# Token rows gathered as half rows on 128 partitions, and a mixture-of-experts loop whose first weight piece is used in two halves

## The reference, cut to what matters

```python
logits = x2 @ w_router + b_router
top_v, top_i = lax.top_k(logits, 4)
gates = softmax(top_v)
# the 1280 (token, expert) pairs are sorted by expert and padded to blocks;
# for every block of rows xb with its expert e:
gu = xb @ w_gu[e] + b_gu[e]                     # (rows, 1024) @ (1024, 2048)
gate = minimum(gu[:, :1024], 7.0)
up = clip(gu[:, 1024:], -7.0, 7.0)
hid = (up + 1.0) * gate * sigmoid(1.702 * gate)
y = hid @ w_dn[e] + b_dn[e]                     # (rows, 1024) @ (1024, 1024)
# out[token] += y * gate of the pair
```

## Time and profile before

| what | us |
|---|---|
| median of 3 runs | 1650.93 |
| lowest and highest run | 1648.24 and 1654.43 |
| the profiled execution, its own time | 1646.45 |
| its span in the profile | 1644.6 |
| TensorE busy | 1488.4 (91%) |
| expert phase: first token transpose to the last down piece | 567.0 to 1617.4 |

### The profile page before, as it was taken

One profiled execution on the slowest core, in us unless ns is written; L12 is line 12 of the kernel. 1 busy time (PEld: TensorE's weight loads), 2 busy tenths in 40 slices (PEclk: granted clock), 3 DMA queues, 4 the chain that ended last, 5 costly groups with the idle time before them and its releaser, 6 DMA issues.

```text
span 1644.6 us, 20052 instructions
## 1 busy us (share of the span) xinstructions
PE 1488.4 (91%) x6990; PEld 690.1 (42%) x6991; DVE 338.2 (21%) x786; ACT 327.9 (20%) x603; POOL 123.5 (8%) x227
## 2 busy tenths in 40 slices
PE   9999999999999898878899988788999886998882
PEld 6676666766774432222233322222333222332221
DVE  3655422333211520100111101001011010011005
ACT  3534423443101111111111111111111110111011
POOL 0200000000000000000010100000101000011000
PEclk9999999999999999989999999899999998999897
DMA  7222132212743499999989999999899999579997
GB/s 271 91 92 79 63 111 79 78 51 103 255 154 154 159 368 413 418 416 409 417 306 376 387 415 416 413 411 418 313 362 397 412 415 404 238 270 407 409 422 233
DMA packets 92391, 477.23 MB, mean 290 GB/s; under 512 B 13015, under 2 KB 16972, under 8 KB 43202
## 3 DMA queue, kind: packets, MB, share of 16 engines
q1 hardware_dynamic: 84040, 461.14, 70.8%
q0 software_dynamic: 7920, 15.45, 2.9%
q10 hardware_dynamic: 394, 0.15, 0.0%
HBM read 471.47 MB, written 15.18 MB: 296 GB/s over the span
## 4 chain that ended last, share of the span: by engine, by line
PE 72%; DMA 20%; DVE 3%; issue 3%; SPq 1%; ACT 0%; ACTq 0%; DVEq 0%; POOL 0%; POOLq 0%
PE bank L622 28%; PE bank L1054 20%; DMA ring<-in_w_gate_up 19%; PE bank L1080 16%; PE bank L626 3%; PE bank L1060 1%; DVE r_kv L1491 1%; DVE r_v L1494 1%; PE bank L903 1%; SPq L579 1%; SPq L586 0%; DMA y_rows<-r_xt,r_qk 0%; PE bank L778 0%; DVE r_c L1494 0%; DVE r_qk L1488 0%
## 5 line engine op out<-in xcount | busy, mean ns | idle before, releaser
L1054 PE MATMUL bank<-ring,r_kv 128*64 128x512 f32 x2128 | 510.3, 627 | 99.5 <-DMA ring<-in_w_gate_up 98.8
L1054 PEld LDWEIGHTS bank<-ring,r_kv 128*64 128x64 f32 x2128 | 153.0, 143 | 401.5 <-issue 296.0
L1080 PE MATMUL bank<-ring,r_kv 128*64 128x512 f32 x1216 | 283.5, 609 | 0.7 <-ACT r_kv L1164 0.7
L622 PE MATMUL bank<-r_xt,ring 128*128 128x320 f32 (+2 forms) x848 | 241.7, 440 | 0.9 <-ACT r_o L1164 0.9
L1488 DVE TENSOR_SCALAR r_kv<-bank 128x512 f32<-128x512 f32 (+1 forms) x78 | 53.6, 687 | 913.2 <-PE bank L1060 911.9
L622 PEld LDWEIGHTS bank<-r_xt,ring 128*128 128x128 f32 x848 | 158.3, 190 | 71.0 <-issue 5.0
L1080 PEld LDWEIGHTS bank<-ring,r_kv 128*64 128x64 f32 x1216 | 90.8, 144 | 193.8 <-issue 192.9
L1164 ACT ACTIVATE r_xt<-bank 128x512 f32<-128x512 f32 x38 | 22.7, 597 | 513.7 <-PE bank L1080 513.7
L1434 ACT ACTIVATE r_o<-r_kv 128x512 f32<-128x512 f32 x38 | 24.0, 632 | 310.3 <-DVE r_kv L1488 310.3
L626 PEld LDWEIGHTS bank<-const,r_v 64*128 64x128 f32 (+3 forms) x512 | 48.4, 156 | 75.0 <-DVE r_v L1494 42.8
L1060 PE MATMUL bank<-ring,r_kv 128*64 128x512 f32 x304 | 71.6, 592 | 0.0
(11 more groups left out here) (258 smaller groups left out, 907.5 us busy)
## 6 DMA issues: line engine op xcount, KB each, us to landing
ring<-in_w_gate_up SPq DMA_DIRECT2D x256, 1024.0 KB, 18.6
ring<-in_w_down SPq DMA_DIRECT2D x128, 1024.0 KB, 14.9
ring<-in_w_in SPq DMA_DIRECT2D x12, 2048.0 KB, 8.4
ring<-in_w_proj_b SPq DMA_DIRECT2D x2, 2048.0 KB, 9.1
ring<-in_w_proj_a SPq DMA_DIRECT2D x2, 2048.0 KB, 9.8
ring<-in_w_out SPq DMA_DIRECT2D x2, 2048.0 KB, 8.0
ring<-y_rows SPq DMA_DIRECT2D x8, 512.0 KB, 11.3
ring<-in_w_uq SPq DMA_DIRECT2D x2, 1152.0 KB, 9.2
```

The costliest lines, as they stand in the source:

```text
L622: ins = pe.matmul(out, l, r, start=(n == 0), stop=(n == len(pairs) - 1), **kw)
L1054: ins = pe.matmul(half(gate_bank if q < 2 else up_bank, q % 2), xg[:, k, :], w[:, 512 * q:512 * q + 512], start=False, stop=False, skip_gr ...
L1080: ins = pe.matmul(half(out_bank, t), hidT[:, 2 * (j % 2) + s, BLK * h:BLK * h + BLK], w[:, s, 512 * t:512 * t + 512], start=(j == 0 and s ...
```

## The change

Four things are changed together.

- **The gather.** `xrow` becomes 128 partitions by 512 columns. Slot s has the first half of its row on partition s and the second half on partition 64 + s; the index table gets one entry for every partition (2 times the token, plus 1 for the upper 64), and the gather takes rows of 2 KB.
- **The token transposes.** 4 transposes of 128 by 128 take the place of 8 of 64 by 128. The bank then holds, for each of four 128-column groups, the slots' lower half and upper half side by side; `xg` is indexed by (k % 4, k // 4), so that every matmul still reads 64 adjacent columns.
- **The order on TensorE.** Behind `bias`, the two gate matmuls of piece 0 (`first_gate`, with the waits for `m_xg` and for the weights) stand ahead of `hidden_turned`, and its two up matmuls (`first_up`) behind it.
- **`pick` on VectorE** is made at the start of a turn, when piece 0 of the block is through, and no longer between `gt` and `up`.

```diff
-        xg = r3(r_kv[:, 0:512], 8)
+        xg = r_kv[:, 0:512].rearrange("p (k h s) -> p k h s", k=4, h=2)
-        xrow = r_v[0:BLK, 1216:2240]
+        xrow = r_v[:, 1216:1728]
+        x_halves_dram = x_rows_dram.rearrange("t (h d) -> (t h) d", h=2)
...
-                for k in range(8):
-                    ins = turn(xt_bank[:, BLK * k:BLK * k + BLK], xrow[:, 128 * k:128 * k + 128])
+                for k in range(4):
+                    ins = turn(xt_bank[:, 128 * k:128 * k + 128], xrow[:, 128 * k:128 * k + 128])
...
+            def first_gate(e):
+                pe.wait_ge(up_in[0], 16 * e + 16)
+                for t in range(2):
+                    pe.matmul(half(gate_bank, t), xg[:, 0, 0, :], up_w(0)[:, 512 * t:512 * t + 512],
+                              start=False, stop=False, skip_group_check=True)
+            def first_up():
+                for t in range(2):
+                    ins = pe.matmul(half(up_bank, t), xg[:, 0, 0, :], up_w(0)[:, 1024 + 512 * t:1536 + 512 * t],
+                                    start=False, stop=False, skip_group_check=True)
+                ins.then_inc(m_up, 1)
...
                 bias(b + 1)
+                pe.wait_ge(m_xg, b + 2)
+                first_gate(e1)
                 hidden_turned(b)
-                pe.wait_ge(m_xg, b + 2)
-                gate_up(0, e1)
+                first_up()
...
             with dve.Fori(0, nb) as b:
+                dve.wait_ge(m_up, 8 * b + 1)
+                ts(pick, lane, be[:, bass.ds(dve.snap(b + 1), 1)], ALU.is_equal).then_inc(m_pick, 1)
                 dve.wait_ge(m_gate, b + 1)
                 ts(gt, banks[2][:, :], LIMIT, ALU.min).then_inc(m_gt, 1)
-                ts(pick, lane, be[:, bass.ds(dve.snap(b + 1), 1)], ALU.is_equal).then_inc(m_pick, 1)
...
-                pool.indirect_dma_start(xrow, None, x_rows_dram[:, :],
-                                        bass.IndirectOffsetOnAxis(ap=column[0:BLK, :].bitcast(U32), axis=0),
-                                        bounds_check=NQ - 1, oob_is_err=False).then_inc(m_xrow, 16)
+                pool.indirect_dma_start(xrow, None, x_halves_dram,
+                                        bass.IndirectOffsetOnAxis(ap=column.bitcast(U32), axis=0),
+                                        bounds_check=2 * NQ - 1, oob_is_err=False).then_inc(m_xrow, 16)
```

More of the change, by code:

```diff
@@ L51 @@
                   ("mask", NT), ("expert", NE), ("block", NB1), ("lane", 1),
-                  ("slot", BLK), ("thr", 6), ("pad", 3), ("tok4", 12)]:
+                  ("slot", BLK), ("thr", 6), ("pad", 4), ("tok4", 12)]:
     CONST_AT[_name] = (_at, _n)
@@ L86, in constants @@
     put("tok4", TOPK * (first + p - NQ))
-    put("pad", np.concatenate([TOPK * NQ + p % BLK, 2 * (TOPK * NQ + p % BLK) + p // BLK,
-                               np.where(p % BLK, 2 * NQ, NQ - 1)], axis=1))
+    put("pad", np.concatenate([TOPK * NQ + p % BLK - 1.5, 2 * (TOPK * NQ + p % BLK) + p // BLK,
+                               np.where(p % BLK, 16 * NQ, TOPK * (NQ - 1)), p // BLK], axis=1))
     return c
@@ L1053, in gate_up @@
                     for q in range(4):
-                        ins = pe.matmul(half(gate_bank if q < 2 else up_bank, q % 2), xg[:, k, :],
+                        ins = pe.matmul(half(gate_bank if q < 2 else up_bank, q % 2), xg[:, k % 4, k // 4, :],
                                         w[:, 512 * q:512 * q + 512], start=False, stop=False, skip_group_check=True)
@@ L1059, in gate_up @@
                     for t in range(2):
-                        ins = pe.matmul(half(bank_, t), xg[:, 7, :], w[:, 512 * (q0 + t):512 * (q0 + t) + 512],
+                        ins = pe.matmul(half(bank_, t), xg[:, 3, 1, :], w[:, 512 * (q0 + t):512 * (q0 + t) + 512],
                                         start=False, stop=True, skip_group_check=True)
@@ L1425, in tokens @@
             def tokens():
-                return copy(xg[:, :, :], banks[0][:, :].rearrange("p (k s) -> p k s", k=8))
+                return copy(r_kv[:, 0:512], banks[0][:, :])
             act.wait_ge(m_gath, 1)
@@ L1853, in _ @@
             tab = bank(("tab",))
-            step(ts(idxf[0:BLK, 0, :], tab[0:BLK, 0:NB1], cst("pad", BLK)[:, 0:1], ALU.add, 0.25, ALU.mult))
-            step(ts(idxf[0:BLK, 0, :], idxf[0:BLK, 0, :], -0.375, ALU.add, 12582912.0, ALU.add))
-            step(ts(idxf[0:BLK, 0, :], idxf[0:BLK, 0, :], 12582912.0, ALU.subtract, cst("pad", BLK)[:, 2:3], ALU.min))
-            signal(dve.tensor_copy(idx[0:BLK, 0, :].bitcast(U32), idxf[0:BLK, 0, :]), idx_set, 1)
+            step(ts(idxf[:, 0, :], tab[:, 0:NB1], cst("pad")[:, 0:1], ALU.add, cst("pad")[:, 2:3], ALU.min))
+            step(ts(idxf[:, 0, :], idxf[:, 0, :], 0.5, ALU.mult, 25165824.0, ALU.add))
+            step(ts(idxf[:, 0, :], idxf[:, 0, :], 25165824.0, ALU.subtract, cst("pad")[:, 3:4], ALU.add))
+            signal(dve.tensor_copy(idx[:, 0, :].bitcast(U32), idxf[:, 0, :]), idx_set, 1)
             filled(dve, "be")
```

## The result

The changed kernel takes 1638.45 us (median of 4 runs, 1636.98 to 1639.21) and the kernel before, in the same session, 1651.4. The ratio is 0.9921, with a 95% interval from 0.9900 to 0.9941. In a later session it was measured again beside its variants: 1637.36 us, ratio 0.9922 (0.9901 to 0.9943). The forecast was 1639 us, in a range from 1631 to 1651.

A forecast was written before the change was run, and what follows sets the result against it. The expert loop was taken as paced by DMA weight loads in some stretches and by TensorE in four others. Terms -4.3 + 2.8 - 10 = -11.5 us took the median of 1650.93 to 1639 us, range 1631 to 1651.

The forecast's parts named there:

- The gather, forecast -10: DMA-paced stretches: the 128-partition gather takes away most of the weight stream's loss around 24 gathers, -10 us.
- the bounds: Gather term: 0 if the loss is of the direction DRAM to SBUF, -14 us if of the 64-partition width.
- rival (b): Gathers on the DMA engines: the changed gather loses as little as the scatter; 1635 us, chance 0.13.
- The prediction's estimate from its figure: DMA ports into SBUF: at 27.2 GB/s a port, a full gather takes 1.2 us before and 0.6 after.
- The turning sections, forecast -4.3: TensorE between bias and down piece 0: gate half fills the hidden-row wait, 10 sections by 0.43 us, -4.3 us.
- The transposes behind the wait, forecast +2.8: Start of four TensorE stretches: hidden transposes move behind piece 0's landing, 4 times 0.7 us; ends +2.0 and +5.6.
- The steps at no cost: Token transposes, pick's move and GpSimd's gather issue (at most 1 us more, under cover) were taken to cost nothing.
- Rival (a): Gathers on the DMA engines: loss stays, coming from scattered DRAM rows read beside a full stream; 1649 us, chance 0.24.
- (c): Gathers on the DMA engines: loss goes by the element, so twice the elements double it, +14; 1663 us, chance 0.08.
- (d): TensorE order: late hidden rows or hidT eat the 0.43 us, four waits cost 1.4 each; 1646 us, chance 0.05.
- the half-clock part: Four waits beginning TensorE stretches: moved transposes cost 1.4 us each at half clock; rival's whole chance 0.05.
- The signs: Large-gather windows 385 GB/s or more, DMA-paced turns 0.3 to 0.6 us shorter, TensorE-paced 23.25, 19 piece-0 waits no shorter.

The follow-up runs named there:

- after_again: The changed kernel, unchanged, measured again in a later session beside its variants: 1637.36 us, ratio 0.9922.
- e1_gather: The kernel before with only the gather on 128 partitions and its four token transposes, order and pick as before: 1638.71 us, ratio 0.9935.
- e2_order: The kernel before with only first_gate, first_up and the new place of pick, gather on 64 partitions as before: 1650.35 us, ratio 0.9998.
- e5_no_rows: The kernel before with slot numbers of blocks 2 and up out of range, so gathers are issued but move nothing: 1627.28 us, ratio 0.9853.
- e7_whole_piece: The changed kernel with piece 0 not cut in two, whole ahead of the hidden transposes: 1650.99 us, ratio 1.0002 to the kernel before.
- e3_wide_rows: The kernel before with 4 KB rows gathered to partitions 0-31 and 96-127, token transposes as eight identity matmuls: 1653.04 us, ratio 1.0019.
- e8_matmul_turn: The kernel before, gather on 64 partitions, with its eight token transposes written as eight matmuls with the identity: 1659.72 us, ratio 1.0048.
- e10_downs_first: The kernel before with the 128-partition gather and all four down pieces ahead of gate_up 0 to 7 of the next block: 1639.73 us, ratio 0.9929.
- e11_split_copy: 128-partition gather and all four down pieces ahead of gate_up 0 to 7, plus hidT copied in two halves from two banks: 1633.99 us, ratio 0.9901.
- e4_narrow_halves: The kernel before with each gather made two gathers of 64 half rows of 2 KB, both into partitions 0 to 63: 1651.23 us, ratio 1.0007.

## Why the forecast was right, and where not

The end was split at nearly the same places as in the prediction. T is the landing of the last awaited piece 0 of a run (the first T is where the first DMA-paced stretch begins), and E the issue of piece 1 at a restart, 6.9 us behind the issue of piece 0 that the prediction took. In before they stand at 642.71, 799.24, 904.65, 1126.85, 1232.29, 1394.59, 1453.62, 1584.20, with the end at 1644.60. Each difference is the stretch's length minus that of before, in us:

| stretches | after | after_again | e1_gather | e2_order | e5_no_rows | e7_whole_piece |
|---|---|---|---|---|---|---|
| four paced by DMA | -3.2, -3.0, -3.7, -2.4 | -3.9, -4.0, -3.8, -2.1 | -2.9, -3.0, -3.5, -1.9 | -0.4, -1.0, +0.1, +0.3 | -5.5, -6.0, -5.9, -4.4 | -3.1, -2.5, -3.0, -1.9 |
| sum | -12.4 | -13.8 | -11.3 | -1.0 | -21.8 | -10.5 |
| four paced by TensorE, sum | +1.8 | +1.3 | +0.3 | +2.7 | +0.7 | +13.0 |
| up to the first T | +3.3 | +3.4 | +3.1 | +4.1 | +2.5 | +2.6 |

The same three sums (DMA, TensorE, up to the first T) are -8.4, +8.5, +5.8 for e3_wide_rows and +0.8, +10.2, +5.4 for its control e8_matmul_turn, -12.5, +4.2, +2.7 for e10_downs_first and -13.3, -0.5, -0.2 for e11_split_copy.

**The gather, forecast -10, measured -11.3 to -13.8.** The mechanism was the right one as far as it was tested, and the bounds held: the loss was of a gather 64 partitions wide, and nearly all of it is gone. Whether the width of the issue counts or the partitions that are written, which the prediction took for one thing, is open (e3_wide_rows). By windows, a large gather loses 0.84 us beyond its bytes before ((421 - 362) / 421 of 6 us) and 0.03 after, a small one 0.30 and 0.05; by landings 0.96 and 0.07, 0.43 and 0.13. The size was too small because I went by the gathers' own bytes over again (8.2 us), and discounted the 14 us that the windows had shown. (The 3.4 MB behind the 8.2 us are those of 26 gathers; the 24 carry 3.2.) The prediction's rival (b), that the gather would lose as little as the scatter, describes the DMA engines better than the forecast did.

The page "SBUF — State Buffer" of the Trainium skill, section "Door 1: The DMA port swizzle", gives the sign for the large gathers of all four gather experiments: partitions 0 to 63 reach half the ports, and partitions 0 to 31 with 96 to 127 reach both halves. For the small gathers of e3_wide_rows, which by it reach half the ports, the late pieces (0.37 us) agree with it and the weight packets (316 ns for 391) do not. The prediction's estimate from its figure, an excess of 0.6 us for a full gather, is below what is measured: the windows of the four full ones in before (340 to 356 GB/s) lose 1.0 us each. So they did not agree in size, as the prediction had it. That the loss falls on the other queue's packets is in the DMA view above. The traces do not tell which port or which engine a packet used.

**The turning sections, forecast -4.3, measured about -1.5.** This is the term that was mis-sized: 10 sections by 0.15 us and not by 0.43. The wait of 0.23 us did go, and the gate half stands in its place. But a group takes longer than I had put it down for when the kind of work changes in front of it or behind it: inside a piece one matmul follows the other after 0.43 us, behind transposes or a bias the second matmul follows after 0.47, and the transposes follow a gate matmul after 0.52. Bias to gate half is 1.02 us and I had 0.93; gate half to transposes is 1.01 and I had 0.86; the up half takes 0.91, the upper end of what I had, and I had gone by 0.86. Only the transposes were right, 0.68. Together that is 0.29 us too little. I had cut a piece of 1.72 us in two equal halves and not asked what a cut costs. This could be read from before: a piece behind the transposes is 1.94 long in the earlier trace rows, and 1.88 behind other pieces, and the token transposes at 821.57 start 0.52 us behind the last matmul of the piece ahead of them (821.05).

**The transposes behind the wait, forecast +2.8 (ends +2.0 and +5.6).** The four TensorE stretches came to +1.8 and +1.3 in all. With -1.5 of the sections, the term was +2.8 to +3.3; in e2_order, with +2.7 in all, it was 4.2. But the single stretches do not bear out that the transposes only push other work out of the time at half clock. In the last one the granted clock is 0.50 from 1575.8 to 1582.6 in after and from 1580.7 to 1587.5 in before, so 5.6 us of it lie behind the landing where it was 3.3, and from the landing to the next token transposes it is 1.79 us longer. In after_again it is 0.95 longer, and in e1_gather, which moves nothing, 0.97. The end is no later for it (-0.1), since what follows the last weight piece is 1.87 us shorter in after; why, the traces do not show. So the size of the term came out, and its account is not shown.

**The steps at no cost** held: `pick` at 828.07 is awaited by no one, the gather takes 1.04 us to issue where it took 0.96, and the copy of `hidT` has 0.21 us to spare. e7_whole_piece shows what this last cover is worth: 13.6 us.

**The sum.** With what was measured it is -1.5 + 2.8 - 13 = -11.7 (13 by the medians of e1_gather and its before), and the forecast was -11.5; the medians of after and before differ by 12.95. The time was right by luck in part, because two errors of about 3 us cancelled; the order, for which I had -1.5, is worth nothing that can be measured alone (e2_order), and its TensorE stretches got longer, not shorter. Rival (a) has fallen by e1_gather, e3_wide_rows and after itself, (c) by e1_gather and e4_narrow_halves, though two of its elements went in one packet, and of (d) only the half-clock part was seen.

**The signs.** Windows about large gathers passed 385 GB/s (419), and the fourteen turns inside DMA-paced stretches average 30.54 us where they took 31.12, within the 0.3 to 0.6 I had named. Turns paced by TensorE missed the 23.25. The 19 waits for piece 0 are a little shorter (94.2 us for 98.8), where I had said longer or as long: the transposes that were moved behind a wait stand ahead of the next one, so TensorE's work between two landings is only 0.15 us shorter, while the landings come 0.6 us closer.

## What to carry to other kernels

Where an indirect gather runs beside a saturated weight stream, let it go out over all 128 partitions, even if each row has to be cut in two. Look for its price in the rate of the stream's own packets, not in the gather's bytes or its queue. When a section is reordered to fill a wait, take the price of each group from a row in which the same kind of work stands in front of it, and before a slot is freed sooner, follow what SP's fixed order frees later for it.

## What the runs showed of the hardware that was not expected

- A 64-partition gather of 0.26 MB makes the other queue's packets take 20% longer per MB over a window of 6 us, while all 16 engines count as busy (share 1.02, 340 GB/s). About large gathers a weight packet of 8 KB takes 452 ns while the rows are on their way, where it takes 323 beside the 128-partition gather and 313 with none. Cutting its rows from 4 to 2 KB leaves the number of its packets at 80, 64 of them with 4 KB of rows.
- A gather issued over 128 partitions whose few rows land in partitions 0 to 31 alone slows no packet of the stream (316 ns, 417 GB/s), and yet makes a weight piece 0.37 us late beyond its bytes (e3_wide_rows).
- The same eight 64-column turnings cost 0.71 us as transposes and 2.00 us as matmuls with the identity, in 16 instructions for 8.
- TensorE was granted 0.50 (the level of 1.2 GHz) about each of the 19 single waits of about 5 us for piece 0. In e10_downs_first and e11_split_copy, where such time is spread over waits of about 0.6 us (at most 1.3) between pieces, it kept 1.00 (2.4 GHz) through the loop to its last block, and the mean was 0.988 and 0.989 where after had 0.950. What that gave by itself was not measured.
